# One core, a mixing layer and a mixture of experts: identity products added on TensorE, one weight load issued earlier, and the far lists stored by slot

## What is computed

```python
def step(S, inp):                       # the recurrence, token by token
    r_t, w_t, k_t, v_t, kk_t, a_t = inp
    sa = jnp.einsum('bhij,bhj->bhi', S, -kk_t)
    S = (S * w_t[:, :, None, :] + sa[..., :, None] * (kk_t * a_t)[:, :, None, :]
         + v_t[..., :, None] * k_t[..., None, :])
    return S, jnp.einsum('bhij,bhj->bhi', S, r_t)
...
gp, gi = lax.top_k(grp_prob, 1)         # the experts
ev, ei = lax.top_k(in_grp, TOP_K_IN_GROUP)
wts = jax.nn.softmax(ev, axis=-1) * gp
...
hg = jnp.einsum('nd,edf->nef', hf, w_gate)
hu = jnp.einsum('nd,edf->nef', hf, w_up)
act = jax.nn.silu(hg) * hu * gates[:, :, None].astype(h.dtype)
y = jnp.einsum('nef,efd->nd', act, w_down)
```

## Time and profile before

| | |
|---|---|
| median of 3 runs | 959.68 us (959.66 to 966.05) |
| the profiled execution, its time | 969.34 us |
| its span on the core | 967.6 us |
| mean granted clock of TensorE in it | 0.945 |
| TensorE busy | 890.7 us (92%) |
| VectorE, ScalarE, GpSimd busy | 456.3, 253.8, 277.5 us |
| DMA moved | 136.31 MB |

### The profile page before, as it was taken

The page is one execution under the profiler, slowest core; times in us unless marked ns, Lnnn a source line. Parts: engine busy times, 40 slices in busy tenths (PEclk is TensorE's granted clock), DMA queues, the critical chain, the costliest instruction groups (busy, mean ns, idle before and its releaser), DMA issues.

```text
span 967.6 us, 17223 instructions
## 1 busy us (share of the span) xinstructions
PE 890.7 (92%) x7090; PEld 609.3 (63%) x7090; DVE 456.3 (47%) x1135; ACT 253.8 (26%) x608; POOL 277.5 (29%) x264
## 2 busy tenths in 40 slices
PE   5989999999999998999998999999999999998860
PEld 5554445655544447888887755555698888886740
DVE  4820477666721125556564324434465555554434
ACT  5220212222200012534434211221312222222203
POOL 4800000000599101433325010000023666543222
PEclk9899999999999998989799899999989999999995
DMA  9823434443010104000004037121479988887548
GB/s 345 237 89 107 132 109 151 130 153 109 23 44 23 43 14 161 4 3 3 2 3 154 3 137 298 44 87 44 150 267 344 296 275 270 268 260 239 157 111 347
DMA packets 81284, 136.31 MB, mean 141 GB/s; under 512 B 18781, under 2 KB 52794, under 8 KB 81210
## 3 DMA queue, kind: packets, MB, share of 16 engines
q1 hardware_dynamic: 71050, 118.44, 34.7%
q0 software_dynamic: 10160, 16.82, 7.2%
HBM read 123.65 MB, written 29.92 MB: 159 GB/s over the span
## 4 chain that ended last, share of the span: by engine, by line
PE 82%; DMA 6%; DVE 4%; SPq 3%; issue 2%; ACT 2%; POOL 0%; DVEq 0%; POOLq 0%; ACTq 0%
PE bank L751 78%; DMA REG_W<-in_moe_w_down 3%; SPq L473 3%; PE bank L1240 2%; DVE REG_P L2063 1%; DMA y_d<-REG_Y,tbl 1%; PE bank L863 1%; DMA REG_P<-y_d 1%; PE bank L1172 1%; PE bank L988 1%; ACT REG_S L1287 1%; DVE REG_P L1832 1%; DMA REG_Y<-in_x 1%; DMA y_d<-REG_Y,idx 0%; DVE REG_P L1565 0%
## 5 line engine op out<-in xcount | busy, mean ns | idle before, releaser
L751 PE MATMUL bank<-REG_W 128*128 128x512 f32 (+1 forms) x864 | 286.3, 527 | 6.8 <-DVE REG_P L1676 2.5
L751 PEld LDWEIGHTS bank<-REG_W 128*128 128x128 f32 (+1 forms) x864 | 126.3, 187 | 151.0 <-issue 146.4
L751 PE MATMUL bank<-REG_W,REG_Y 128*128 128x512 f32 x256 | 121.5, 613 | 1.7 <-DVE REG_Y L2019 1.1
L1287 ACT ACTIVATE REG_P<-bank 128x256 f32<-128x256 f32 (+2 forms) x126 | 57.1, 460 | 189.7 <-PE bank L751 150.9
L751 PE MATMUL bank<-REG_P 64*64 64x64 f32 (+1 forms) x2816 | 88.4, 224 | 6.8 <-issue 2.9
L751 PEld LDWEIGHTS bank<-REG_P 64*64 64x64 f32 x2816 | 82.5, 137 | 12.0 <-issue 5.2
L751 PE MATMUL bank<-REG_Y,REG_W 128*128 128x128 f32 (+1 forms) x640 | 70.8, 280 | 6.9 <-DMA REG_W<-in_moe_w_down 5.1
L751 PEld LDWEIGHTS bank<-REG_Y,REG_W 128*128 128x128 f32 (+1 forms) x640 | 67.3, 184 | 13.7 <-issue 11.2
L751 PEld LDWEIGHTS bank<-REG_W,REG_Y 128*128 128x128 f32 x256 | 46.7, 195 | 45.9 <-issue 45.8
L1287 ACT ACTIVATE REG_Y<-bank,mod,s 128x128 f32<-128x128 f32 x132 | 49.6, 456 | 84.3 <-PE bank L1240 84.3
L751 PE MATMUL bank<-REG_Y,REG_P 128*128 128x128 f32 x496 | 58.3, 275 | 3.4 <-DMA REG_P<-in_moe_w_down 1.8
(11 more groups left out here) (281 smaller groups left out, 1198.2 us busy)
## 6 DMA issues: line engine op xcount, KB each, us to landing
REG_P<-in_w_ada SPq DMA_DIRECT2D x18, 1024.0 KB, 6.2
REG_W<-in_w_in SPq DMA_DIRECT2D x17, 512.0 KB
REG_P<-in_moe_w_gate SPq DMA_DIRECT2D x17, 512.0 KB, 8.9
REG_W<-in_moe_w_gate SPq DMA_DIRECT2D x16, 512.0 KB, 6.9
REG_W<-in_moe_w_up SPq DMA_DIRECT2D x16, 512.0 KB, 10.9
REG_W<-in_moe_w_down SPq DMA_DIRECT2D x16, 512.0 KB, 20.0
REG_P<-in_moe_w_up SPq DMA_DIRECT2D x14, 512.0 KB, 12.2
REG_P<-in_w_ada SPq DMA_DIRECT2D x3, 2048.0 KB, 12.4
```

The costliest lines, as they stand in the source:

```text
L751: return pe.matmul(o_, l, r, start=start, stop=stop, skip_group_check=True)
L1287: return act.activation(o_, i_, f, **kw)
```

## The change

Five things change in the text of the kernel.

- `beside` gets a second argument, the PSUM bank, and is defined ahead of the front of the turns.
- Identity products: eight stand before the wait that ends in `w_go`, and behind it seven are left of 14. Eight are added between `norm_flip` and `norm_back`. In a turn one follows each state step, except where the router's bias stands, and two more follow the last step of each turn but the last. In the last tile's routing four stand before the transposes, four between transposes and lists, none between lists and logits (there were four), and seven in place of six before the last list. In all there are 138 where there were 104.
- The weights of expert 8 are issued before SP's waits for the first two gathers; those of 9 and 10 still behind them.
- `far_d` is read as (slot, tile) in place of (tile, slot), so that the 15 entries of a slot lie together.
- VectorE computes `far_at` to fit: it divides the place by 128 by comparing it with 1 to 7, which makes four instructions more.

```diff
             for n in range(2):
                 sp.wait_ge(s_st[n], 16 * NT // 2)
+            load_expert(8, TURN[8], s_w[8])
             for b in range(2):
                 sp.wait_ge(s_gx[b], 16)
-            for e in range(8, RING):
+            for e in range(9, RING):
                 load_expert(e, TURN[e], s_w[e])
...
-                    sp.dma_start(tbl[:, E:TILES, :], far_d.rearrange("(t p) c -> p t c", p=P)).then_inc(s["far_ld"], 16)
+                    sp.dma_start(tbl[:, E:TILES, :], far_d.rearrange("(p t) c -> p t c", t=OVT)).then_inc(s["far_ld"], 16)
...
+            def beside(n, bank):
+                for _ in range(n):
+                    mm(PS[bank][:, 0:P], ident[:, :], ident[:, :])
+
+            beside(8, 4)
             pe.wait_ge(s["proj_act"], NB)
...
                         if not more and n == 0:
                             router_bias(4 * c, 4 * c + 4)
...
-            beside(14)
+                        else:
+                            beside(1, 4)
+                if more:
+                    beside(2, 4)
+
+            beside(7, 3)
             loras(0)
-            beside(8)
+            beside(8, 3)
             norm_sums(front_norm(0), sq)
-            beside(8)
+            beside(8, 3)
             norm_flip(front_norm(0))
+            beside(8, 3)
             norm_back(front_norm(0))
-            beside(18)
+            beside(18, 3)
...
+            beside(4, 0)
             x1_turned(NT - 1)
+            beside(4, 0)
             listed(NT - 2)
-            beside(4)
             logits(NT - 1)
-            beside(16)
+            beside(16, 0)
             ranks(NT - 1)
-            beside(6)
+            beside(7, 0)
             listed(NT - 1)
...
-            ch.step(stt(rt["obs"], rt["obs"], float(CAP), places, ALU.mult, ALU.add))
-            stt(far_at[:, :], rt["obs"], float(-CAP), rt["far"], ALU.add, ALU.add).then_inc(s["rt_n"], 1)
+            lane = rt["nov"][:, 0:2 * NT]
...
+            ch.step(ts(lane, places, 1.0 / CAP, None, ALU.mult))
+            ch.step(tt(steps, lane.unsqueeze(2).to_broadcast([P, 2 * NT, NT - 1]),
+                       i32[:, 1:NT].unsqueeze(1).to_broadcast([P, 2 * NT, NT - 1]), ALU.is_ge))
+            ch.step(dve.tensor_reduce(lane, steps, AX.X, ALU.add))
+            ch.step(stt(lane, lane, 1.0 - CAP * OVT, rt["obs"], ALU.mult, ALU.add))
+            ch.step(stt(rt["obs"], places, float(OVT), lane, ALU.mult, ALU.add))
+            stt(far_at[:, :], rt["obs"], -1.0, rt["far"], ALU.add, ALU.add).then_inc(s["rt_n"], 1)
```

More of the change, by code:

```diff
@@ L1139, in turn @@
                             router_bias(4 * c, 4 * c + 4)
-            def beside(n):
-                for _ in range(n):
-                    mm(PS[3][:, 0:P], ident[:, :], ident[:, :])
-            beside(14)
+                        else:
[3 more added lines that the diff above has]
+            beside(7, 3)
             loras(0)
-            beside(8)
+            beside(8, 3)
             norm_sums(front_norm(0), sq)
-            beside(8)
+            beside(8, 3)
             norm_flip(front_norm(0))
+            beside(8, 3)
             norm_back(front_norm(0))
-            beside(18)
+            beside(18, 3)
             for m in range(TURNS):
@@ L1260, in ex_dn @@
                 last.then_inc(s[pre + "dn"], 1)
-            beside(24)
+            beside(24, 3)
             ex_t(0, 0, 16, wait_free=False)
-            beside(6)
+            beside(6, 3)
             ex_t(1, 1, 16)
@@ L2003, in _ @@
             ch.wait()
-            ch.step(stt(rt["obs"], rt["obs"], float(CAP), places, ALU.mult, ALU.add))
-            stt(far_at[:, :], rt["obs"], float(-CAP), rt["far"], ALU.add, ALU.add).then_inc(s["rt_n"], 1)
+            lane = rt["nov"][:, 0:2 * NT]
+            steps = rt["cmp"][:, 0:2 * NT * (NT - 1)].rearrange("p (a i) -> p a i", i=NT - 1)
+            ch.step(ts(lane, places, 1.0 / CAP, None, ALU.mult))
[5 more added lines that the diff above has]
+            stt(far_at[:, :], rt["obs"], -1.0, rt["far"], ALU.add, ALU.add).then_inc(s["rt_n"], 1)
             def gate(e):
```

## The result

| | before | after |
|---|---|---|
| median (20 runs each) | 963.39 us (955.28 to 970.37) | 958.08 us (949.91 to 961.68) |
| profiled execution, its span | 967.6 us | 957.0 us |
| mean granted clock of TensorE in it | 0.945 | 0.960 |
| TensorE busy | 890.7 us | 887.2 us |
| DMA packets; of them under 512 B | 81284; 18781 | 79493; 16989 |

The ratio is 0.9944, 95% interval 0.9919 to 0.9970: 5.3 us faster, 0.6%, where 10.6 were forecast. The kernel before is at 963.4 us in 20 runs; the 959.68 shown ahead of the prediction was the median of three.

The account below looks back on a forecast made before the run. TensorE held 82% of the chain of waits, DMA 6%; expert delivery was slower than TensorE's rhythm. Front 3.9, turn ends 1.5, gathers 3.0 and delivery 2.2 sum to 10.6 us: 959.7 to 949.1, range 941 to 958.

Parts of the forecast that it names:

- Front, -3.9: Front of the turns: identity products fill two idle gaps and keep the clock up; first turn starts 3.9 us earlier.
- Turn ends, -1.5: Ends of turns: added products keep TensorE's clock up, gaining 1.5 us, between a 4.5 loss and a 6 gain.
- Routing, -4.1 for the first gather: Last tile's routing: moved products and a higher clock let the first gather issue 4.1 us earlier, at about 707.9.
- For the logits 1.3 us: Last tile's routing: with four products gone ahead of them, the logits start at 697.2 instead of 698.58, 1.3 us.
- I take 6.5 for the first, since the load in front of it is short: First gather beside expert 8's early load: lands in 6.5 us, against 4.4 undisturbed; 3.0 us gain kept for both gathers.
- the idle stretch of 711 to 712: DMA before the first gather: engines at share 0.02 there, so the early load's 1.5 MB would mostly fill a hole.
- The bound of 8.8 us: First gathers: queues alternate packet by packet, so a gather at most about doubles its time, to 8.8 us.
- the 0.7: First gathers under packet-by-packet sharing: low end of the estimated remaining gain, 0.7 to 4.1 us.
- rival 3: Gathers lose what routing wins: they land at 8 to 11 us, delivery gains little; 6.4 us gain, 953.3; chance 0.12.
- Delivery, -4.4, counted as -2.2: Expert weights: earlier delivery gains 4.4 us beyond TensorE's own 3.0; half counted, as ordinary runs may be less late.
- Delivery starts the long 9 us rhythm with one expert less in the queue: Expert stage: experts arrive 9.0 us apart; the early load completes the first eleven at about 730, 7.4 us earlier.
- Lists by slot, 0: Far lists' read: fewer, longer runs count 0, gain to 1.5 us; VectorE's added instructions cost up to 1 us uncovered.

Follow-up runs that it names:

- kernel 7: The kernel before with only the identity products at the turns' ends added; 963.74 us, ratio 0.9997.
- 6: The kernel before with only the front's identity products changed (eight before the w_go wait, 7 for 14 behind, eight between norm_flip and norm_back); 957.44 us, ratio 0.9936.
- 8: The kernel before with only the identity products of the last tile's routing changed; 961.24 us, ratio 0.9978.
- 2: The kernel before with only the early load: expert 8's weights issued ahead of the waits for the first two gathers; 965.04 us, ratio 1.0027.
- experiment 9: The changed kernel with expert 9's weights also issued ahead of the waits for the first two gathers; 959.70 us, ratio 0.9981 to the kernel before.
- Experiment 10: The changed kernel with expert 8's weights behind both gathers again and only an eighth of experts 8 and 9's weights loaded; 953.94 us, ratio 0.9919 to before.
- Experiment 11: The changed kernel with expert 8's weights behind both gathers again and an eighth of experts 11 to 31's down weights loaded; 942.09 us, ratio 0.9810 to before.
- experiment 3: The kernel before with all the identity product changes, without the early load or the lists by slot; 954.98 us, ratio 0.9928.
- 5: The late load: the changed kernel with expert 8's weights issued behind the first two gathers again; 953.12 us, ratio 0.9891 to the kernel before.
- 12: The changed kernel with expert 8's weights behind both gathers again and each expert's down weights on their own semaphore; 954.71 us, ratio 0.9927 to before.
- 4: The changed kernel with the far lists read tile by tile, as before; 958.74 us, ratio 0.9965 to the kernel before.
- 1: The kernel before with only the far lists by slot, including VectorE's four more instructions; 961.31 us, ratio 0.9985.

## Why the prediction was too high

It promised 10.6 us of gain; 5.3 were measured.

**Front, -3.9: right.** 3.9 us in the trace, by the steps given: both gaps covered, the clock up, the return and the 18 products at full rate. In the medians it is 6.2 us (3.9 to 8.5), and what the rest would come from is not shown. It carries the change.

**Turn ends, -1.5: nothing.** 0.3 us (-2.8 to 3.3). The saving for a kept clock was counted as if a product kept it; in the kernel after, the clock still falls ahead of a turn:

```profile
500.00:504.00 4.00, 4.00 (x50) 3.31 (x48) 2.83 (x6) 1.38 (x6) 0.00 (x0) 0.50 0.01 2
```

The price at the low clock was too small as well. Two state steps of the kernel before, then two of kernel 7, all at the low clock:

```profile
461.70 0.70 PE L751 MATMUL bank<-REG_S 64*64 64x64 f32 x8 [0.19 <-ACT REG_S L1287]
463.02 0.69 PE L751 MATMUL bank<-REG_S 64*64 64x64 f32 x8 [0.19 <-ACT REG_S L1287]
...
503.70 0.69 PE L751 MATMUL bank<-REG_S 64*64 64x64 f32 x8
505.47 0.69 PE L751 MATMUL bank<-REG_S 64*64 64x64 f32 x8
```

A step takes 1.32 us without a product and 1.77 with one, 0.45 more where the prediction had 0.22. From the first step to the next turn's pairs it is 5.6 us (460.39 to 466.03, before) against 7.9 (501.93 to 509.87, kernel 7), 2.3 for 1.5. At the upper clock both kernels take 4.9 us: there the product is covered, as forecast.

**Routing, -4.1 for the first gather: 2.1 us (loss of 1.0 to gain of 5.2) alone.** For the logits 1.3 us were forecast and about 1 is the products' own work (experiments 6 to 8); the saving from the clock was counted on the earlier trace rows, which only some executions of the kernel before show. From the start of the logits to the gather's issue kernels 2, 6 and 7 take 10.5 us and the kernel after 10.6, for 13.4 before.

**Gathers behind the early load: sharing taken too lightly.** The step "I take 6.5 for the first, since the load in front of it is short" failed. It left 3.0 of the routing's 4.1 us, a loss of 1.1 to the load; 4.4 were lost (first gate product 12.71 us after the first gather's issue, for 8.31 with the late load). 3.5 of them are the landing, 8.1 us for 4.6, and 0.9 the low clock behind the wait, which the sum did not have. The prediction did bring the gather forward, to 707.9, beside the load from 708.1, but took the room for both from the idle stretch of 711 to 712. That stretch was there because the routing was slow: expert 7's down load, issued at 701.06, had landed 10.7 us later, just before the gather's issue at 711.96. In the kernel after the gather goes out at 695.26, 6.8 us behind expert 7's down load (688.48) instead of 10.9, and the early load keeps the DMA engines full until 702. The bound of 8.8 us that the prediction drew from the Trainium skill ("DMA: Bandwidth & Descriptors", "Queues, rings and completion order") was nearer than my 6.5, but it is no bound: 11.2 us in experiment 9 is more than double 5.1. Nor does the 0.7 beside it follow from its terms, since 4.1 - 4.4 is -0.3. What came is rival 3, "the gathers lose what the routing wins", which had 0.12.

**Delivery, -4.4, counted as -2.2: nothing.** The step "Delivery starts the long 9 us rhythm with one expert less in the queue" failed. 9.0 us was 170.6 us over 19 experts, a mean over two regimes. SP in the kernel before:

```profile
754.71 0.33 SPq L473 DMA_DIRECT2D REG_P<-in_moe_w_gate  x1
...
760.87 0.33 SPq L473 DMA_DIRECT2D REG_W<-in_moe_w_gate  x1
...
842.99 2.65 SPq L473 DMA_DIRECT2D REG_P<-in_moe_w_gate  x1
...
850.79 1.95 SPq L473 DMA_DIRECT2D REG_W<-in_moe_w_gate  x1
```

Until about 770 a load goes out when a place comes free, every 6.16 us; a head start there mostly makes SP wait. Experiment 10 took 2.75 MB out of the start and won nothing in the medians (1.7 us of the stage in its trace). Experiment 11 took 9.6 MB out of the rest and won 12.1 us of the stage; the amounts differ too, so it is the issue and landing times of 10, not this pair alone, that show where the head start goes. Late weights do cost what the prediction thought; when delivery starts hardly sets how late they are. In the kernel after it is the same: expert 30's down load is issued 159.2 us behind the first gate product for 165.9 before, and the product that needs it still waits, 33.0 us behind that issue. Why the landing takes longer when the issue is earlier was not settled.

**Lists by slot, 0: right.** SP's long issue is gone, with 1.4 us (loss of 1.7 to gain of 4.6) in the medians: a cost of VectorE's added instructions cannot be told from none.

**Sum.** Identity products -6.9 (experiment 3), early load +3.8, lists -1.4: 4.5 us, beside 5.3 measured. The largest error lies in routing, gathers and delivery together: 3.0 + 2.2 us of gain were forecast, and 2.1 less 3.8, a loss of 1.7, was measured. The base was off too: 959.68 stood for 963.4. The gain of 10.6 us in profiled executions agrees with the forecast by chance, as 9.7 of it lie where the forecast had 2 to 3.

## What to carry to other kernels

An idle stretch in which an added transfer is to hide must be looked for in the schedule after the change, not before it: the part that speeds up the work ahead may close it, and the low clock behind a new wait belongs to its price. A mean rhythm between two far points should be split at the issues: where loads go out in the consumer's rhythm, buffers set it, and an earlier start is paid back as waiting. And the price of low clock in one profiled execution belongs to that execution until a second one shows it in the same place.

## What was not expected of the hardware

- A kernel's first gather of 128 rows landed in 4.3 to 4.9 us with the DMA engines full at its issue but no new load behind (experiments 3, 5, 6, 8, 10, 12), and in 7.5 to 8.3 with expert 8's 1.5 MB issued around it (2, 4, 9; 8.1 in the kernel after by TensorE's wait). With 3 MB issued around them (9) the later gathers took up to 11.2.
- With many loads outstanding SP's issue of one mostly takes 2 to 8 us for 0.33 to 0.43 otherwise, and behind the list read in runs of 8 bytes one issue took 18 to 27 us.
- The granted clock fell in other places from run to run with the same code: from turn 3's start to the end of the last logits it took 183 to 191 us (before, 1, 2, 6).
